# Two MoE layers of a decoder trunk: order and place of the expert weight loads, a gathered first pair, and a second round split into gate and up

## The reference

```python
for l in range(DEPTH):                        # 2 layers
    h = h + mixer(rmsnorm(h, norm_mix[l]))    # mLSTM in layer 0, attention in layer 1
    h = h + hier_moe(rmsnorm(h, norm_ffn[l]), ...)

def hier_moe(h, ...):
    top_g = argmax(x @ w_group + b_group)     # best of 4 groups
    top_v, top_i = top_k(router logits of that group, 2)
    gates = one_hot(...) * softmax(top_v) * p_g
    for each expert e:
        y += (silu(x @ w_gate[e]) * (x @ w_up[e]) * gates[:, e]) @ w_down[e]
```

## Time and profile before

| | us |
|---|---|
| median of 3 runs (lowest, highest) | 593.41 (592.73, 596.48) |
| the profiled execution: its time / its span in the trace | 594.13 / 592.3 |
| layer 0: second half of the projection, up to `gate_up(0)` | about 145 to 170.9 |
| layer 0: `gate_up(0)` to the end of the MoE | 170.9 to 296.1 |
| layer 1: `gate_up(0)` to the end | 464 to 592 |

### The profile page before, as it was taken

One profiled execution on the slowest core, in us unless ns is written; L12 is line 12 of the kernel. 1 busy time (PEld: TensorE's weight loads), 2 busy tenths in 40 slices (PEclk: granted clock), 3 DMA queues, 4 the chain that ended last, 5 costly groups with the idle time before them and its releaser, 6 DMA issues.

```text
span 592.3 us, 9235 instructions
## 1 busy us (share of the span) xinstructions
PE 571.6 (97%) x3690; PEld 369.4 (62%) x3690; DVE 212.5 (36%) x616; ACT 146.7 (25%) x409; POOL 41.9 (7%) x91
## 2 busy tenths in 40 slices
PE   8999999999999999999989999999999999998996
PEld 4687878889863454444466777777899533332331
DVE  3353113331224744444464333433422246121222
ACT  3313113331132211111253333333403312111110
POOL 7010000000001100000003110001000011000000
PEclk9999999999999999999999999999999999999999
DMA  9989630030396999999999514030404969999981
GB/s 285 349 190 350 211 132 1 4 138 1 112 387 234 397 419 420 421 421 418 356 349 348 190 62 153 20 123 1 142 1 153 413 252 411 420 421 422 419 357 72
DMA packets 58504, 147.74 MB, mean 249 GB/s; under 512 B 10044, under 2 KB 42876, under 8 KB 46172
## 3 DMA queue, kind: packets, MB, share of 16 engines
q1 hardware_dynamic: 54112, 136.06, 61.5%
q0 software_dynamic: 2880, 10.42, 4.7%
q10 hardware_dynamic: 1468, 0.65, 0.5%
HBM read 143.89 MB, written 3.23 MB: 248 GB/s over the span
## 4 chain that ended last, share of the span: by engine, by line
PE 78%; DMA 16%; DVE 3%; ACT 1%; SPq 1%; issue 1%; DVEq 0%
PE bank L1534 29%; DMA ring<-in_moe_w_up 16%; PE bank L1849 14%; PE bank L1669 10%; PE bank L1876 4%; PE bank L1806 2%; PE bank L1638 2%; PE bank L2055 1%; PE bank L2040 1%; PE bank L1903 1%; PE bank L2086 1%; PE bank L1900 1%; PE bank L1550 1%; SPq L427 1%; PE bank L2082 1%; PE bank L1691 1%
## 5 line engine op out<-in xcount | busy, mean ns | idle before, releaser
L1534 PE MATMUL bank<-hxT,ring 128*128 128x272 f32 x576 | 138.2, 394 | 1.4 <-ACT hxT L882 0.9
L1534 PEld LDWEIGHTS bank<-hxT,ring 128*128 128x128 f32 x576 | 107.8, 190 | 23.6 <-issue 2.6
L1849 PE MATMUL bank<-ring,gate_area 128*64 128x512 f32 (+1 forms) x608 | 114.9, 595 | 5.7 <-DMA ring<-in_moe_w_up 5.7
L1849 PEld LDWEIGHTS bank<-ring,gate_area 128*64 128x64 f32 (+1 forms) x608 | 36.2, 125 | 60.7 <-issue 59.7
L1669 PE MATMUL bank<-tok,ring 128*128 128x128 f32 (+1 forms) x512 | 63.2, 280 | 0.1
L1669 PEld LDWEIGHTS bank<-tok,ring 128*128 128x128 f32 x512 | 60.2, 191 | 1.9 <-issue 1.5
L1876 PE MATMUL bank<-ring,gate_area 128*32 128x512 f32 x480 | 58.9, 595 | 0.0
L1218 DVE TENSOR_TENSOR qk_area<-qk_area,bank 128x256 f32<-128x256 f32 x16 | 6.7, 421 | 86.0 <-ACT qk_area L827 86.0
L1876 PEld LDWEIGHTS bank<-ring,gate_area 128*32 128x32 f32 x480 | 15.6, 110 | 32.8 <-issue 31.9
L827 ACT ACTIVATE qk_area<-bank 128x256 f32<-128x256 f32 x16 | 6.1, 383 | 105.4 <-PE bank L1849 105.4
L1534 PE MATMUL bank<-big,ring 128*128 128x256 f32 x128 | 29.2, 380 | 0.0
(11 more groups left out here) (304 smaller groups left out, 662.5 us busy)
## 6 DMA issues: line engine op xcount, KB each, us to landing
ring<-in_moe_w_gate SPq DMA_DIRECT2D x30, 1024.0 KB, 15.4
ring<-in_moe_w_up SPq DMA_DIRECT2D x30, 1024.0 KB, 17.6
ring<-in_moe_w_down SPq DMA_DIRECT2D x30, 1024.0 KB, 20.5
ring<-in_m_w_in SPq DMA_DIRECT2D x11, 1024.0 KB, 12.4
ring<-in_kv_w SPq DMA_DIRECT2D x8, 1024.0 KB, 12.0
ring<-in_m_w_out SPq DMA_DIRECT2D x4, 1024.0 KB, 12.7
ring<-in_f_w_q SPq DMA_DIRECT2D x4, 1024.0 KB, 12.0
ring<-in_f_w_o SPq DMA_DIRECT2D x4, 1024.0 KB, 6.6
```

The costliest lines, as they stand in the source:

```text
L1534: ins = pe.matmul(bank[c % 2][:, 0:n], w[:, k, half * P:half * P + P], x[:, k, 0:n], start=(k == 0), stop=(k == KB - 1))
L1849: ins = pe.matmul(bank[1][s, :], xgT[b % 2][:, q, s], unit_gate_up(g, q), start=(q == 0), stop=(q == KB - 1))
```

## The change

It has five parts.

1. **A fourth spare unit** (`BESIDE`): both down units of the pair b = 2 now lie beside the ring. The fourth lies in the tile `big`, and for its place `comb` shrinks from 8 buffers to 3, so `combine_weights(b)` waits for `combine(b - 3)`.
2. **First gather in layer 0**: `rows_picked(0, ...)` goes. TensorE computes the row numbers of b = 0 before m = 24 (`rows_of_slots(1, (0,))`), DVE turns them into `idx`, POOL gathers the rows from DRAM as soon as the first two tiles are written, and TensorE transposes them before m = 49 and m = 55. Layer 1 keeps `rows_picked`.
3. **Order of the loads** (`load_moe`): the four down units of round 0 come ahead of the spare units, and in layer 0 the spare loads wait for the first gather. Then come four gate units, then the four up units beside them, then the rest.
4. **Round 1 in two passes**: `gate_up(1)` runs all 32 gate products of 256 columns, signals `g_done`, and then all 32 up products. The slots of the four gate units are free at `g_done`. `rows_of_slots(3, ...)` moves from q = 6 to q = 5 of the first pass.
5. **More banks**: in the last `combine` of layer 0 the third block (i = 2) goes to banks 2 and 3, which needs no wait for DVE.

```diff
-        BESIDE = [[u_ + 2 * PU, u_ + 2 * PU + 1, u_ + 2 * PU + 4] for u_ in U_MOE]
+        BESIDE = [[u_ + 2 * PU + i for i in (0, 1, 4, 5)] for u_ in U_MOE]
...
+                            if old == g and b < 2:
+                                sp.wait_ge(sem("g_done"), l + 1)
+                            elif old in (g, u_):
                                 sp.wait_ge(*in_layer("gu_done", l, max(b + 1, 2)))
...
                 gate_up(0)
                 gate_up(1)
-                if l == 0:
-                    gate_up(2, (0,))
                 down(0)
                 down(1)
-                if l == 1:
-                    gate_up(2, (0,))
-                down(2, (0,))
-                for b in range(2, NPAIR):
-                    gate_up(b, [par for par in (0, 1) if not beside(b, par)])
-                    if b >= 3:
-                        down(b - 1, [par for par in (0, 1) if not beside(b - 1, par)])
+                if l == 0:
+                    sp.wait_ge(sem("x_in0"), 16)
+                gate_up(2, (0,))
+                down(2)
+                for kinds in ((0,), (1,)):
+                    for b, pars in ((2, (1,)), (3, (0, 1)), (4, (0,))):
+                        gate_up(b, pars, kinds)
+                for b in range(4, NPAIR):
+                    gate_up(b, (1,) if b == 4 else (0, 1))
+                    if b >= 4:
+                        down(b - 1)
...
+                    if l == 0 and p == 0:
+                        pool.wait_ge(sem("xs_written"), 32)
+                        pool.wait_ge(sem("idx_ready"), 1)
+                        pool.indirect_dma_start(
+                            out=xg[0], out_offset=None, in_=xs[0][0:META + P, :],
+                            in_offset=bass.IndirectOffsetOnAxis(ap=idx[:, 0:1], axis=0)).then_inc(sem("x_in0"), 16)
...
+                    if b >= NY:
+                        dve.wait_ge(*in_layer("c_done", l, all_combined(l, b - NY)))
...
-                x_evac(0)
-                add_out(l, 1, 0)
+                if l == 0:
+                    row_of_slot(l, 0, 1, 1)
+                    add_out(l, 1, 0)
+                    x_evac(0)
...
-                            if m == 25:
+                            if l == 0 and m == 24:
+                                rows_of_slots(1, (0,))
+                            if l == 1 and m == 25:
                                 rows_picked(0, 0)
...
+                            if l == 0 and m == 49:
+                                rows_to_cols(0, 0)
+                            if l == 0 and m == 55:
+                                rows_to_cols(0, 1)
...
+                            if b == 1:
+                                ins = pe.matmul(bank[1][s, 0:FE], xgT[1][:, q, s], unit_gate_up(g, q)[:, 0, :],
+                                                start=(q == 0), stop=(q == KB - 1), skip_group_check=True)
+                                continue
...
+                    if b == 1:
+                        ins.then_inc(sem("g_done"), 1)
+                        for q in range(KB):
+                            for i, (g, _, _) in enumerate(units):
+                                s = slice(w * i, w * (i + 1))
+                                ins = pe.matmul(bank[1][s, FE:2 * FE], xgT[1][:, q, s], unit_gate_up(g, q)[:, 1, :],
+                                                start=False, stop=(q == KB - 1), skip_group_check=True)
```

More of the change, by code:

```diff
@@ L261, in unit_flat @@
                     i = BESIDE[l].index(s)
[L262 removed]
+                    return (hxT[:, 1 - l, 0:2 * D], hxT[:, 2 - l, 0:2 * D], tok_flat[:, D:3 * D], big[:, 4 * D:6 * D])[i]
             return ring[:, s % RING, :]
@@ L360, in combined, with combine_bank @@
             return per * b + i + 1 if b < 2 else 2 * per * (b - 1) + 2 * i + part + 1
+        def combine_bank(b, i, part):
+            if b == NPAIR - 1 and i == 2:
+                return 2 + part
+            return 4 + part + 2 * (i % 2) if not (b == NPAIR - 1 and i == 3) else 4 + part
         def all_combined(l, b):
@@ L422, in load_moe, with gate_up @@
             def load_moe(l):
-                def gate_up(b, pars=(0, 1)):
+                def gate_up(b, pars=(0, 1), kinds=(0, 1)):
                     for par in pars:
-                        for s, w in zip(expert_units(l, b, par), (io["moe_w_gate"], io["moe_w_up"])):
+                        for kind in kinds:
+                            s, w = expert_units(l, b, par)[kind], (io["moe_w_gate"], io["moe_w_up"])[kind]
                             slot_is_free(s)
@@ L1126, in first_rows @@
                 dve.wait_ge(*in_layer("eall_ready", l, p + 1))
-                first = pick[:, t0:t1, :].rearrange("p t (e s) -> p t e s", e=EPG)
+                first = (sel if (l, p) == (0, 0) else pick)[:, t0:t1, 0:P].rearrange("p t (e s) -> p t e s", e=EPG)
                 places = iota_f[:, p * P:(p + 1) * P].rearrange("p (e s) -> p e s", e=EPG)
@@ L1736, in rows_of_slots @@
                     pe.wait_ge(*in_layer("sel_ready", l, part))
+                    ts = part_tiles(l, 0) if part == 1 else tiles
                     for i in blocks:
                         at = (i % 4) * P
-                        for m, (t, rows, _) in enumerate(tiles):
+                        for m, (t, rows, _) in enumerate(ts):
                             ins = pe.matmul(bank[4][:, IDX + i:IDX + i + 1], sel[0:rows, t, at:at + P],
-                                            tcol_of(l, t)[0:rows, :], start=False, stop=(m == nt - 1),
+                                            tcol_of(l, t)[0:rows, :], start=False, stop=(m == len(ts) - 1),
                                             skip_group_check=True)
@@ L1812, in rows_to_cols @@
                     if half == 0:
-                        pe.wait_ge(*in_layer(f"x_in{b % NXG}", l, 16 * ((b - 2) // NXG + 1)))
-                        pe.wait_ge(*in_layer("xT_read", l, b))
+                        n_in = len([o for o in ((0,) if l == 0 else ()) + tuple(range(2, b + 1)) if o % NXG == b % NXG])
+                        pe.wait_ge(*in_layer(f"x_in{b % NXG}", l, 16 * n_in))
+                        if b:
+                            pe.wait_ge(*in_layer("xT_read", l, b))
                         if b == 2:
@@ L1842, in gate_up @@
                             positions(1)
-                        if b == 1 and q == 6:
+                        if b == 1 and q == 5:
                             rows_of_slots(3, (2, 3))
@@ L1899, in combine @@
                                     j = 2 * i + c
[L1900 to L1901 removed]
+                                    ins = pe.matmul(bank[combine_bank(b, i, part)][:, c * w:(c + 1) * w], y[s, j * P:(j + 1) * P],
+                                                    comb[s, b % NY, c0:c0 + w], start=True, stop=True, skip_group_check=True)
                                 else:
[L1903 removed]
+                                    ins = pe.matmul(bank[4 + 2 * part + half][:, :], comb[s, b % NY, c0 - off:c0 - off + w],
                                                     y[s, half * HALF:(half + 1) * HALF], start=(b == part),
```

43 lines of the change are left out of this document (21 added, 22 removed).

## The result

The changed kernel took 606.26 us in the median of 4 runs (605.55 to 606.86), against 593.41 (592.73 to 596.48) before. Over all runs the ratio is 1.0204, with a 95% interval of 1.0162 to 1.0245. Forecast were 598.0 us and a range of 592 to 603. The profiled execution took 606.48 us with a span of 604.7; the sum had given 598.6 for it.

The account below looks back on a forecast made before the run. TensorE, busy 97% of the span, was taken as the bound, with DMA nearly equal. Layer 0 5.7 us slower and layer 1 1.2 us faster put 4.5 us on 594.13: 598.6, stated as 598 us, range 592 to 603.

Parts of the forecast that it names:

- The gather's landing and the wait at m = 49: Layer 0, first gather: rows land 8.9 us after issue, at 168.0, and TensorE waits 8.0 us.
- The rival of the quick gather: Layer 0: the gather lands after 4.9 us, TensorE waits 4.0 us, the clock holds, total 591; chance 0.16.
- the cold start: Layer 0, behind the wait at m = 49: TensorE restarts at the lower clock level, which costs 2.6 us before `gate_up(0)`.
- slower: the gather meets a full queue: Layer 0: the gather lands after 11.5 us, total 600.6, or 602.6 with `gate_up(2)` at the late end; chance 0.29.
- Part 4: Round 1: two passes take 7.1 us like one, the selector's wait is 0.5 us, gates are asked for 3.1 us sooner.
- The landing of the first up unit in layer 0: Now fifth in the queue, it lets `gate_up(2)` begin at 210.5 against 202.65 before, 7.9 us late.
- The same in layer 1: First up unit lands at 497.7, so `gate_up(2)` waits 2.9 us; layer 1 is still 1.2 us faster in all.
- The clock in front of `gate_up(2)`: The clock falls only after some 4.4 us without work, so no fall was charged at `gate_up(2)` in either layer.
- The waits of the pairs go: MoE pairs: TensorE's weight waits vanish, 1.7 us in layer 0 and 4.1 us in layer 1.
- The sum: Whole kernel: layer 0 5.7 us slower, layer 1 1.2 us faster, so 4.5 us on 594.13 gives 598.6.
- The bound of the range: Whole kernel: 592 for the quick gather with some of the middle, up to 603 for a late one with a dry queue.
- three signs that I named for being wrong: Changed trace: gather landing before 165, pairs still waiting for weights, or half-width products taking clearly more than 7.1 us together.

Follow-up runs that it names:

- e6: The changed kernel with its first gather undone, the first up unit third in the queue, and round 1 in one pass without `g_done`: 595.26 us.
- e8: e7 with the transposes before m = 60 and 63 and ACT's squares ahead of its part of the scaling: 583.25 us.
- e7: The changed kernel with the first up unit third in the queue and SP's wait for the gather ahead of round 0's four down units: 588.81 us.
- e1: The changed kernel with part 2 undone, so layer 0 picks its first rows by matmul again: 601.54 us.

## Why the prediction was wrong, point by point

The direction was right, and the sum was 7.9 us too small (606.48 against 598.6). Two steps failed, both at `gate_up(2)`. The wait for the first up unit was put at 2.0 and 2.9 us and measured 4.35 and 6.48. And the clock was held up behind these waits, where it fell behind both. Step by step:

- **The gather's landing and the wait at m = 49: right.** Predicted were a landing 8.9 us after the issue and a wait of 8.0 us; it was 9.3 and 9.16. The rival of the quick gather fell. `gate_up(0)` came at 176.67, forecast 176.5. That it is so close is partly luck: the transposes began at 168.81 and not 168.1, and from there to `gate_up(0)` it took 7.9 us, where 5.8 and 2.6 for the cold start make 8.4.
- **The rival "slower: the gather meets a full queue"** had its landing at 169.4 or later. It landed at 168.8, and even its later value was 602.6, so the result on its side came by another way, the terms below.
- **Part 4: right.** The two passes of round 1 took 7.2 us, as long as the one of full width before (both without the row numbers and the wait ahead of them), the selector's wait was 0.36 us (0.5 forecast), and the gates went out at 193.47 (193.1 forecast).
- **The landing of the first up unit in layer 0: the value was off, the mechanism right.** I took 210.5, the middle between 208.5, where TensorE is ready, and 212.5, today's landing put off by three units. It was 212.93, at the late bound, and TensorE was ready at 208.7. Reading today's row and adding what now stands ahead was better than counting units at the full rate. `gate_up(2)` was 10.4 us late, not 7.9: 2.5 us missed.
- **The same in layer 1: undersized.** I counted six units of 2.5 us from the end of the spare loads (482.7), that is 15 us. They ended at 493.44 in the new times, 1.1 us later than forecast (483.8 in the old times, with the 9.65 us by which `gate_up(0)` of layer 1 is late taken off), and the first up unit landed at 510.89: 17.4 us, which is seven units at the full rate. The wait was 6.48 us, not 2.9: 3.6 missed. Two gathers that I had not counted, of b = 4 and b = 5, were issued at 504.17 and 505.41 and lie in that stretch; how much of them had passed before 510.89 was not told apart, so this stays a candidate.
- **The clock in front of `gate_up(2)`: the second step that failed.** I let it fall only for waits of more than 4.4 us, from a single row at the end of the kernel, and so charged it once. It fell 2.4 us after the last matmul in layer 0 and 3.6 us in layer 1, and `gate_up(2)` took 9.52 and 9.03 us instead of 7.1: 2.4 and 1.9 us that no term held. In part this follows from the sizes of the waits: a wait of 6.48 us I would have charged by my own rule, one of 4.35 us not. Whether the clock would have fallen behind the 2.0 and 2.9 us of the forecast is not shown. The trace of before has one wait of that kind, 2.27 us, and there it held; in e6 it fell with waits of 2.56 and 2.69 us. The Trainium skill (page "TensorE: Matmul & The Clock Gate", section "Loop structure matters more than you think") shows a DMA wait of 8 us after which the array runs at half rate; the waits of 4.35 and 6.48 us here were followed by the same. The wait of 2.27 us and its clock, in the kernel before:

```profile
537.77 2.80 PE L1849 MATMUL bank<-ring,gate_area 128*64 128x512 f32 x12 [2.27 <-DMA ring<-in_moe_w_up]
```

```profile
535.60:537.70 2.10, 0.00 (x0) 0.00 (x0) 0.00 (x0) 0.02 (x1) 0.00 (x0) 1.00 1.02 425
```

- **The waits of the pairs go: right.** 1.7 and 4.1 us are 0.0, and of DVE's 1.1 us 0.5 are gone (no run takes part 5 out alone). The loads were never late again, and it paid no more than these 6.3 us.
- **The sum.** Missed were 2.5 + 2.4 us in layer 0 (0.4 less by small terms) and 3.6 + 1.9 in layer 1, together 10.0. Against it stand 2.0 us outside the MoE that the changed kernel was faster by, 0.5 in the attention stage and 1.5 behind the last product, in the store of the result. That makes 8, the 7.9 within rounding. The change touches neither place; in another execution these 2.0 us may be missing.
- **The bound of the range.** Its upper end held a late gather, a dry queue and one fall, but not further falls. The waits that I forecast myself, 2.0 and 2.9 us, were taken as too short for one, without a row for 2.9 us or more. Of the three signs that I named for being wrong (a landing before 165, waits of the pairs, slow half-width products) none came: they did not cover the two steps that failed.

## What to carry to other kernels

When loads are sorted by kind instead of by use, work out for the first product of the new order how many bytes stand ahead of its last operand, other queues' transfers included; a gain on later waits is capped by what those waits are now, while the new one is not. Price a wait of TensorE twice, with the clock held and with a fall behind it: in these traces all nine waits of 2.56 us or more were followed by a fall (1.9 to 2.4 us more for the 32 records of `gate_up(2)` in the changed kernel), the one of 2.27 us in the kernel before was not, and no row tells what lies between. Moving work from TensorE to a gather paid here only when both held: few bytes queued with it, and its use late in the program (e8, not e7).

## What was not expected of the hardware

- The granted clock fell at no fixed time after the last matmul: 1.6 us (e1), 2.4, 3.6 and 3.7 us (changed kernel), 4.4 us (end of the kernel before). In e6 it also fell once at 158.1 with TensorE busy before it and through it.
- Runs of one kernel differ in it: the mean granted clock is 0.984 in the profiled run of e6 (598.40 us) and 0.993 in its fastest (592.75 us), 0.992 in the fastest run of e1 (597.11 us) and 0.983 in its slowest (603.68 us).
- It then stayed at the lower level for 10.2 us (changed kernel, from 163.4), 6.8 us (in front of `gate_up(2)` in the changed kernel, e1 and e6) or 3.4 us (e7, from 164.0), whether or not TensorE had work again in the meantime:

```profile
164.10:167.30 3.20, 3.05 (x15) 3.05 (x16) 0.69 (x1) 0.00 (x0) 0.00 (x0) 0.50 0.63 200
167.50:172.00 4.50, 4.50 (x53) 3.56 (x51) 0.55 (x1) 1.14 (x4) 0.00 (x0) 1.00 0.99 419
```

- The longer wait did not have the longer fall: 4.26 us in e7 with 3.4 us at the lower level, 2.69 us in e6 with 6.8 us at it. What sets this was not told apart.
